# Up and down projections in three 256-column products per k-tile, and short matmuls ahead of chosen units

## The reference

```python
h = rmsnorm(x, norm_mix)
parts = split(h @ w_in)                      # 2048 x 14612: three mixers and gates
y_a, y_b, y_c = deltanet(..), mlstm(..), stick_breaking(..)
merged = gate_a * (y_a @ wb_a) + gate_b * (y_b @ wb_b) + gate_c * (y_c @ wb_c)
x = x + merged @ w_out
x = x + cross_attention(rmsnorm(x), rmsnorm(mem))   # wq, wkv, wo, four heads
up = causal_dwconv(rmsnorm(x) @ w_up, w_conv)       # 2048 x 11264, width 3
g, u = split(up)
out = x + (silu(g) * u) @ w_down                    # 5632 x 2048
```

## Time and profile before

| | |
|---|---|
| median of 3 runs | 2000.78 us (1995.47 to 2001.36) |
| profiled execution, its time | 2001.66 us |
| its span, first to last instruction | 1999.8 us |
| mean granted TensorE clock | 0.999 |
| TensorE busy | 1985.7 us, 99% |
| VectorE busy | 1216.7 us, 61% |
| ScalarE busy | 891.6 us, 45% |
| HBM traffic | 191 GB/s over the span |

### The profile page before, as it was taken

One profiled execution on the slowest core, in us unless ns is written; L12 is line 12 of the kernel. 1 busy time (PEld: TensorE's weight loads), 2 busy tenths in 40 slices (PEclk: granted clock), 3 DMA queues, 4 the chain that ended last, 5 costly groups with the idle time before them and its releaser, 6 DMA issues.

```text
span 1999.8 us, 34706 instructions
## 1 busy us (share of the span) xinstructions
PE 1985.7 (99%) x14790; PEld 1895.3 (95%) x14790; DVE 1216.7 (61%) x1352; ACT 891.6 (45%) x877; POOL 40.3 (2%) x62
## 2 busy tenths in 40 slices
PE   8999999999999999999999999999999999999999
PEld 8999999999999999999999999888888888888888
DVE  5677645445454476676655345777777777754444
ACT  5445434434374333455434444544444444433333
POOL 1000100000000000000000000000000000000000
PEclk9999999999999999999999999999999999999999
DMA  8665744665557756565554455665656565567564
GB/s 268 212 200 196 226 159 143 211 198 169 181 167 267 238 190 217 177 196 170 191 187 127 151 165 190 214 207 173 204 174 204 175 202 176 176 205 223 185 203 134
DMA packets 356636, 382.65 MB, mean 191 GB/s; under 512 B 8143, under 2 KB 351603, under 8 KB 355123
## 3 DMA queue, kind: packets, MB, share of 16 engines
q1 hardware_dynamic: 350947, 353.36, 55.3%
q0 software_dynamic: 5584, 27.70, 3.9%
HBM read 367.47 MB, written 13.58 MB: 191 GB/s over the span
## 4 chain that ended last, share of the span: by engine, by line
PE 98%; DVE 1%; ACT 0%; DMA 0%; issue 0%; SPq 0%; DVEq 0%; ACTq 0%
PE bank L1970 19%; PE bank L1971 18%; PE bank L1972 18%; PE bank L2009 16%; PE bank L2011 8%; PE bank L2485 8%; PE bank L2486 4%; PE bank L2392 1%; PE bank L2411 1%; PE bank L2169 1%; DVE w_lo_home L1139 0%; PE bank L2215 0%; PE bank L2072 0%; PE bank L2163 0%; DMA ident<-in_shape_masks 0%; PE bank L2281 0%
## 5 line engine op out<-in xcount | busy, mean ns | idle before, releaser
L1139 DVE TENSOR_TENSOR w_lo_home<-raw,w_hi_home 128x2048 fp32r<-128x2048 f32 (+1 forms) x349 | 757.0, 2169 | 604.5 <-ACT w_hi_home L547 604.2
L547 ACT ACTIVATE w_hi_home<-raw 128x2048 fp32r<-128x2048 f32 (+2 forms) x359 | 644.8, 1797 | 1047.0 <-PE bank L1972 627.6
L1970 PE MATMUL bank<-x_home,w_hi_home 128*128 128x256 f32 x2304 | 648.8, 282 | 2.0 <-DVE w_lo_home L1139 1.9
L1972 PE MATMUL bank<-x_home,w_lo_home 128*128 128x256 f32 x2304 | 644.4, 280 | 0.0
L1971 PE MATMUL bank<-x_home,w_hi_home 128*128 128x256 f32 x2304 | 644.4, 280 | 0.0
L2009 PE MATMUL bank<-x_home,w_hi_home 128*128 128x512 f32 x1408 | 488.5, 390 | 0.1
L1970 PEld LDWEIGHTS bank<-x_home,w_hi_home 128*128 128x128 f32 x2304 | 435.1, 189 | 2.9 <-issue 1.4
L1972 PEld LDWEIGHTS bank<-x_home,w_lo_home 128*128 128x128 f32 x2304 | 437.0, 190 | 0.0
L1971 PEld LDWEIGHTS bank<-x_home,w_hi_home 128*128 128x128 f32 x2304 | 433.1, 188 | 0.2
L2011 PE MATMUL bank<-x_home,w_lo_home 128*128 128x256 f32 x1408 | 397.1, 282 | 0.0
L2009 PEld LDWEIGHTS bank<-x_home,w_hi_home 128*128 128x128 f32 x1408 | 264.2, 188 | 55.5 <-issue 0.4
(11 more groups left out here) (315 smaller groups left out, 1946.4 us busy)
## 6 DMA issues: line engine op xcount, KB each, us to landing
raw<-in_w_in SPq DMA_DIRECT2D x52, 2048.0 KB, 8.5
raw<-in_ffn_up SPq DMA_DIRECT2D x44, 2048.0 KB, 7.9
raw<-in_ffn_down SPq DMA_DIRECT2D x32, 1408.0 KB, 6.9
raw<-in_xa_wkv SPq DMA_DIRECT2D x16, 2048.0 KB, 9.2
raw<-in_w_br SPq DMA_DIRECT2D x8, 2048.0 KB, 8.3
raw<-in_w_out SPq DMA_DIRECT2D x8, 2048.0 KB, 8.3
raw<-in_xa_wq SPq DMA_DIRECT2D x8, 2048.0 KB, 8.3
raw<-in_xa_wo SPq DMA_DIRECT2D x8, 2048.0 KB, 8.4
```

The costliest lines, as they stand in the source:

```text
L547: return nc.scalar.activation(out_, in_, func, **kw)
L1139: tt(split_out(w_lo, kind, half, at), halves(raw, kind, half, par), split_out(w_hi, kind, half, at).bitcast(f32), ALU.subtract).then_inc(l ...
L1970: mm(o, w[0], x[0], start=start, stop=False)
L1972: return mm(o, w[1], x[0], start=False, stop=stop)
```

## The change

UP and DN compute each k-tile as the other phases do, with `three` into the first 256 columns of the bank, and their weights are put at element 24. `minor`, its copy, the second addition in `finish` and `finish_last`, and three semaphores are gone; the scaling by `rstd` reads PSUM directly. Beside this, a short matmul (`lead_in`) is issued ahead of chosen half units. It multiplies the half unit's first weights and activations and is overwritten by the unit's first product. It has two sizes: `LEAD_WIDE`, 128 stationary and 2 moving columns, and `LEAD_SMALL`, 4 stationary and 16 moving. `SETTLE` is the wide one ahead of a unit's first half and the small one ahead of its second. A pair stands in A (half units 8 and 9), GA (its half units 6 and 7), GC unit 0, BR unit 0, one unit at each of the two calls of `norm_beside` (in WO and K), XO unit 1, UP units 3, 17 and 31, and each of the eight blocks of DN (block 0 ahead of its first unit, the others ahead of their third, after the transposes, with `bank[5]` as the place). BO unit 0 has the small one alone. These are 37 short matmuls.

```diff
-W_OF = {"UP": 0, "DN": 0, "V": 16}
+W_OF = {"V": 16}
+LEAD_WIDE, LEAD_SMALL = (P, 2), (4, 16)
+SETTLE = (LEAD_WIDE, LEAD_SMALL)
+UP_SETTLES = (3, 17, 31)
...
-        minor = sb("minor", [P, 2, SEQ], f32, d_scope)
...
-            def minor_part(j, up):
-                ...
-                for x in range(2):
-                    last = copy(minor[:, x, :], up_bank(par, x)[:, SEQ:2 * SEQ])
-                last.then_inc(f_minor, 1)
...
             def scale_tokens(j, up):
-                dve.wait_ge(f_minor, j * 2 + up + 1)
...
                 for x in range(2):
-                    last = tt(scaled[:, x * SEQ:(x + 1) * SEQ], up_bank(par, x)[:, 0:SEQ], minor[:, x, :], ALU.add)
+                    last = tt(scaled[:, x * SEQ:(x + 1) * SEQ], up_bank(par, x)[:, 0:SEQ], rstd[:, :], ALU.mult)
                 last.then_inc(dve_evac, 1)
-                dve.wait_ge(dve_evac, j * 2 + evacuated("UP", up)[1])
-                tt(scaled.rearrange("p (c s) -> p c s", c=2), scaled.rearrange("p (c s) -> p c s", c=2),
-                   bc(rstd[:, :].unsqueeze(1), [P, 2, SEQ]), ALU.mult).then_inc(f_scaled, 1)
...
             def finish_last(x):
-                tt(part, bank[1 + 2 * x][:, 0:SEQ], x_back[:, 2 * c + x, :], ALU.add).then_inc(dn_main, 1)
-                dve.wait_ge(dn_main, c + 1 + x)
-                tt(part, bank[1 + 2 * x][:, SEQ:2 * SEQ], part, ALU.add).then_inc(dve_evac, 1)
+                tt(part, bank[1 + 2 * x][:, 0:SEQ], x_back[:, 2 * c + x, :], ALU.add).then_inc(dve_evac, 1)
...
+            def lead_in(o, w, x, shape):
+                m, n = shape
+                return mm(o[0:m, 0:n], w[:, 0:m], x[:, 0:n], start=True, stop=True)
...
-                    for k in range(KC if name == "UP" else 0):
-                        ...
-                        mm(o[:, :].rearrange("p (j s) -> p j s", j=2), w_hi_home[:, half, at:at + P], acts[:, :, k, :],
-                           start=k == 0, stop=False)
-                        last = mm(o[:, SEQ:2 * SEQ], w_lo_home[:, half, at:at + P], acts[:, 0, k, :], start=False, stop=k == KC - 1)
+                    out_of = lambda g: up_bank(par, half)[:, 0:SEQ] if name == "UP" else bank[par + 2 * g][:, half * SEQ:(half + 1) * SEQ]
+                    if lead:
+                        lead_in(out_of(0), w_hi_home[:, half, place_of(name):], acts[:, 0, 0, :], lead)
...
             def norm_beside(k, m, acts):
-                product_half(m, acts)
-                product_half(m + 1, acts)
-                product_half(m + 2, acts)
+                leads = dict(zip((m + m % 2, m + m % 2 + 1), SETTLE))
+                for j in range(3):
+                    product_half(m + j, acts, lead=leads.get(m + j))
...
             for m in range(4, 14):
-                product_half(m)
+                product_half(m, lead={8: LEAD_WIDE, 9: LEAD_SMALL}.get(m))
...
+            project("BO", x_hl, 0, 1, leads=(LEAD_SMALL, None))
+            project("GC", x_hl, 0, 1, leads=SETTLE)
+            project("BR", y_hl, 0, 1, leads=SETTLE)
+            project("XO", x_hl, 1, 2, leads=SETTLE)
...
-            project("UP", x_hl, 1)
+            project("UP", x_hl, 1, UP_SETTLES[0])
+            for i, j in zip(UP_SETTLES, UP_SETTLES[1:] + (COUNT["UP"],)):
+                project("UP", x_hl, i, i + 1, leads=SETTLE)
+                project("UP", x_hl, i + 1, j)
...
             def down_pair(c, par):
+                settled = 0 if isinstance(c, int) and c == 0 else 2
...
-                            mm(o[:, :].rearrange("p (j s) -> p j s", j=2), w_hi_home[:, half, at:at + P], x, start=g + k == 0, stop=False)
-                            last = mm(o[:, SEQ:2 * SEQ], w_lo_home[:, half, at:at + P], x[:, 0, :], start=False,
-                                      stop=g * DG + k == FC - 1)
+                            if k == 0 and g == settled:
+                                lead_in((o if g == 0 else bank[5])[:, 0:SEQ], w_hi_home[:, half, at:], x[:, 0, :], SETTLE[half])
+                            w = [t[:, half, at:at + P] for t in (w_hi_home, w_lo_home)]
+                            last = three(o[:, 0:SEQ], w, [x[:, 0, :], x[:, 1, :]], g + k == 0, g * DG + k == FC - 1)
```

More of the change, by code:

```diff
@@ L1093, in _ @@
             hi_half(*half_of(first_half("DN") + 1))
-            minor_part(FC // 2 - 1, 1)
             silu_gate(FC // 2 - 1)
@@ L1940, in finish @@
                               x_back[:, bass.ds(c * 2 + x, 1), :].rearrange("p c s -> p (c s)"), ALU.add)
[L1941 to L1944, removed]
                 last.then_inc(dve_evac, 1)
@@ L1985, in wait_bank, with half_unit @@
                     pe.wait_ge(evac[e], i + (n - 2))
-            def half_unit(name, i, par, hp, half, acts, ready=None, passed=None, parts=None, ks=range(KC)):
+            def half_unit(name, i, par, hp, half, acts, ready=None, passed=None, parts=None, ks=range(KC), lead=None):
                 kind = kind_of[name]
@@ L2001, in half_unit @@
                     cuts = (0, GH, GH + MH, KC) if kind == BR else (0, KC)
-                    for k in range(KC if name == "UP" else 0):
[L2003 to L2008, removed]
-                        mm(o[:, :].rearrange("p (j s) -> p j s", j=2), w_hi_home[:, half, at:at + P], acts[:, :, k, :],
-                           start=k == 0, stop=False)
-                        last = mm(o[:, SEQ:2 * SEQ], w_lo_home[:, half, at:at + P], acts[:, 0, k, :], start=False, stop=k == KC - 1)
-                    for k in ks if name != "UP" else ():
+                    out_of = lambda g: up_bank(par, half)[:, 0:SEQ] if name == "UP" else bank[par + 2 * g][:, half * SEQ:(half + 1) * SEQ]
+                    if lead:
+                        lead_in(out_of(0), w_hi_home[:, half, place_of(name):], acts[:, 0, 0, :], lead)
+                    for k in ks:
                         if parts and k == KC // 2:
@@ L2018, in half_unit @@
                         w = [t[:, half, k * P:(k + 1) * P] for t in (w_hi, w_lo)]
-                        last = three(bank[par + 2 * g][:, half * SEQ:(half + 1) * SEQ], w, [acts[:, j, k, :] for j in range(2)],
+                        last = three(out_of(g), w, [acts[:, j, k, :] for j in range(2)],
                                      k == cuts[g], k + 1 == cuts[g + 1])
@@ L2026, in half_unit, with product_half @@
                     last.then_inc(half_used, 1)
-            def product_half(m, acts=x_hl, ready=None, passed=None, parts=None, ks=range(KC)):
+            def product_half(m, acts=x_hl, ready=None, passed=None, parts=None, ks=range(KC), lead=None):
                 name, i, par, hp, half = half_of(m)
@@ L2032, in product_half, with project @@
                     wait_bank(name, i)
-                half_unit(name, i, par, hp, half, acts, ready, passed, parts, ks)
-            def project(name, acts, start=0, stop=None):
+                half_unit(name, i, par, hp, half, acts, ready, passed, parts, ks, lead)
+            def project(name, acts, start=0, stop=None, leads=(None, None)):
                 def unit(i, par, hp):
@@ L2038, in unit @@
                     for half in range(2):
-                        half_unit(name, i, par, hp, half, acts)
+                        half_unit(name, i, par, hp, half, acts, lead=leads[half])
                 stop = COUNT[name] if stop is None else stop
@@ L2192, in _ @@
             product_half(m + 5)
-            product_half(m + 6)
+            product_half(m + 6, lead=LEAD_WIDE)
             m += 7
-            for _ in range(2 * FIRST_LEVEL - 1):
-                product_half(m)
+            for j in range(2 * FIRST_LEVEL - 1):
+                product_half(m, lead=None if j else LEAD_SMALL)
                 m += 1
@@ L2273, in _ @@
                 to_features(bank[3 + j], j, lambda h, a: S_T[:, a * GH + h, :], y_t)
-            for name in ("BQK", "BV", "BO"):
+            for name in ("BQK", "BV"):
                 project(name, x_hl)
+            project("BO", x_hl, 0, 1, leads=(LEAD_SMALL, None))
+            project("BO", x_hl, 1)
             def scores(b, k, q):
@@ L2347, in _ @@
             product_half(m + 7)
-            project("GC", x_hl)
+            project("GC", x_hl, 0, 1, leads=SETTLE)
+            project("GC", x_hl, 1)
             pe.wait_ge(y_lo, 4)
-            project("BR", y_hl)
+            project("BR", y_hl, 0, 1, leads=SETTLE)
+            project("BR", y_hl, 1)
             m = first_half("WO")
```

12 lines of the change are left out of this document (2 added, 10 removed).

## The result

The changed kernel took 1976.59 us in the median (1975.33 to 1978.79, four runs) against 2000.65 us (1995.47 to 2001.36): 24.1 us faster, a ratio (of the means) of 0.9886 with a 95% interval of 0.9868 to 0.9905. Forecast were 1972 us and a range of 1963 to 2010. The profiled execution took 1976.82 us, its span is 1974.9.

What follows compares the result with a forecast made beforehand. TensorE, 99% busy, was taken as the bound: matmul count times start-to-start distance. Terms -14.3 - 19.0 + 3.7 - 0.4 = -30.0 us from the profiled 2001.66 us gave 1972 us, range 1963 to 2010.

Steps and rivals of the forecast that it cites:

- Two paces that are set by what stands ahead, and then kept: TensorE's stream: 113.2 or 117.7 ns per 256-column matmul; a short block can set either pace, and what follows keeps it.
- The sign that I named, 0.34 us right behind each short matmul: In the changed kernel's stretches, k-tiles of 0.34 us, the fast pace, were to stand right behind each short matmul.
- rival 3: Each short matmul only turns the pace over, so about half the k-tiles are fast: -6.2 us, 1995 us; chance 0.10.
- UP and DN, forecast -14.3 us: Three products instead of two at the fast pace, 339.5 against 346.6 ns: 2016 k-tiles x -7.1 ns = -14.3 us.
- The other half units, forecast -19.0 us: Outside UP and DN, 88 slow halves of 48 matmuls turn fast, 4.5 ns per matmul: -19.0 us, bounds -15.3 and -22.7.
- the 71 halves counted as sure: Slow halves in A, GA, BO, CQK, GC, BR, WO, K and XO, following a pair with only products between: -15.3 us.
- the 34 behind single sums: Halves in WO, K and Q behind single 256-column sums; effect unknown, bounds all and none, so half, 17, were counted.
- The short matmuls, 0.10 us each: The 37 short matmuls lie on TensorE's path: 37 x 0.10 = +3.7 us, bounds 0 and +7.0 us.
- Rival 1: Fast pace only where already seen, with `x_home` as operand, not with `y_hl`, `mem_hl`, `act_hl`: -11.6 us, 1990 us; chance 0.13.
- Rival 2: Short matmuls don't set the pace; UP and DN run slow over 2112 k-tiles: +17.2 us, 2019 us; chance 0.20.
- Its even point, f = 0.60: Rival 2 with no gain elsewhere: 2112 x (6.6 - 13.7 f) + 3.3 = 0; said to decide once over half are slow.
- ScalarE and VectorE, forecast at nothing: Dropped copy and additions, 30 us of VectorE, worth nothing as TensorE never waited; one tail addition fewer, -0.4 us.

Runs made afterwards that it cites:

- experiment 5: The changed kernel with only the pair at XO unit 1, no other short matmuls: 2002.43 us, ratio 1.0012 to the kernel before.
- experiment 6: The changed kernel with one pair in UP, at unit 1, instead of three, and none in DN: 1996.74 us, ratio 0.9989 to the kernel before.
- experiment 9: The changed kernel with one pair in UP, at unit 2, and BO's and A's short matmuls moved: 1978.13 us, ratio 0.9896 to the kernel before.
- experiment 10: The changed kernel with one UP pair, at unit 2, BO's and A's short matmuls moved, no DN pairs: 1973.97 us, ratio 0.9875 to the kernel before.
- experiment 1: The changed kernel without any of its 37 short matmuls, three products kept: 1983.98 us, ratio 0.9925 to the kernel before.
- experiment 2: The kernel before with 15 short matmuls, none in UP and DN, which keep two products per k-tile: 1988.17 us, ratio 0.995 to the kernel before.
- experiment 3: The kernel before with all 37 short matmuls, two products per k-tile and weights at element 0 in UP and DN: 1990.63 us, ratio 0.9961.
- experiment 11: The changed kernel again, unaltered, beside two variants on the same chip: 1977.94 us, ratio 0.9897 to the kernel before.

## Why the prediction was right, and where it was off

**Two paces that are set by what stands ahead, and then kept.** Right for what short matmuls and the sums do, and confirmed at single steps and by experiments 5, 6, 9 and 10. "Kept" needs a limit: waits and single late starts ended the fast pace in some executions and not in others. The sign that I named, 0.34 us right behind each short matmul, holds for the small one alone. What I had not said is that the outcome depends on the pace before: the small one turns it over, so rival 3 describes the small one alone, and the wide one in front is what makes the pair come out the same from either side.

**UP and DN, forecast -14.3 us.** In the profiled executions, the way from the sums to the end of the span went from 729.9 to 721.1 us, -8.8; forecast were -14.3, +2.2 for 22 short ones and -0.4, -12.5 in all. The term that was mis-sized is this one. Slow k-tiles that I had not counted: 64 in UP units 1 and 2, taken as even though the sums leave them slow (64 x 6.6 ns = 0.4 us), and the half unit behind each wide one, 3 x 16 in UP and 8 x 11 in DN, 136 x 13.7 ns = 1.9 us. With a fall between 1755 and 1770 us and 22 x 0.01 us more for the short ones this makes some 3 of the 3.7 us. The rest is in the price: two matmuls taken off each count made the fast k-tile 339.5 ns, while its starts in the traces give 340.0, so that a k-tile is worth 6.6 ns and not 7.1, 1.0 us over 2016, which covers what is left. Experiment 1 shows the products without pairs: from the sums to the last matmul 712.2 us against 726.9, of which 0.4 us is the shorter tail; to the start of the last product 711.2 against 725.4, -14.2 us, where the 2080 k-tiles behind the sums give -14.8 at 7.1 ns and -13.7 at 6.6.

**The other half units, forecast -19.0 us.** With the 15 short ones there at 0.10 us that is -17.5; the profile shows the sums of UP at 1253.7 instead of 1269.9 us, -16.1. By medians it is less, -10.6 in experiment 2, since the profiled execution of before lay near the slow end of its runs. Of the 71 halves counted as sure, A's 6 and BO's 5 did not come; of the 34 behind single sums, where I took half, nearly all did. These two misses have opposite signs, and that the term came out so near is in part luck.

**The short matmuls, 0.10 us each from the earlier trace rows.** Measured 0.11 us, twice. What they cost beside it, a half unit at the slow pace behind each wide one, was in no term of the sum.

**The rivals.** Rival 1 fell: BR with `y_hl`, K with `mem_hl` and DN with `act_hl` all run at 113 ns. Rival 2 said that without an effect of the pairs UP and DN run slow, at 2019 us. That step was wrong as a statement about UP and DN: without any pairs they ran fast, 1984 us, because the long sums happened to turn the pace the right way. Its prices hold: in experiment 5 1508 of the 2112 k-tiles ran slow, and the way from the sums to the last matmul is 732.5 us, 20.3 above experiment 1, where 1508 x 13.7 ns gives 20.7. Its even point, f = 0.60, is the share of fast k-tiles, so it decides once more than 0.4 of them are slow, not half. The Trainium skill ("TensorE: Matmul & The Clock Gate", section "Back-to-back issue gap") gives a matmul's columns at 2.4 GHz and 2.5 ns as the gap of a matmul taken by itself, and says that in a stream the weight loads set the distance too. By that formula 256 columns would be 109.2 ns, an estimate, and three products 2.5 ns more than two. The traces agree that a stream is not bound by it: 113.3 or 117.8 ns, and 768 columns in three products took 340.0 ns, in two 346.6, which is the other direction.

**ScalarE and VectorE, forecast at nothing.** Consistent with TensorE's waits for weights, 3.0 us in three places instead of 1.9 in two. The tail's 0.4 us came: from the start of the last product to the end of the span it is 4.53 us before and 4.08 after, 4.49 and 4.50 in experiments 2 and 3, which keep the second addition, and 4.04 to 4.08 in 1, 5, 6, 9, 10 and 11, which don't.

## What to carry to other kernels

When one engine is busy all the time, divide stretches of its time by the count of its instructions before counting instructions: here one stream ran at 113.3 or 117.7 ns, and 16,000 matmuls times 4.5 ns is more than any single edit gave. A pace that is kept from its start makes distant edits interact, so judge an edit by the pace in each stretch and not by the total, and look at what stands directly behind each foreign block. Where a wait stands in the stream, one trace doesn't settle the pace behind it. And test "the added thing does it" by leaving it out: without the pairs in DN the kernel was faster.

## What the runs showed of the hardware

- A stream of 128 x 128 x 256 matmuls on hi and lo parts has two steady start-to-start distances, 113.3 and 117.8 ns, at the same granted clock of 1.00; with V's weights at element 16 there is a third, 116.7. The pair of a 512-column and a 256-column matmul has one, 346.3 to 347.0 ns by the counts, in the three traces that have it, all with the weights at element 0.
- The fast distance lasted for 6268 matmuls with seven blocks of transposes between (experiment 1), and in CQK through a wait of 1 us in nine traces of thirteen; in the other four it ended there. In K one start 0.03 to 0.04 us late ended it in three traces of eleven.
- A short matmul of 4 stationary and 16 moving columns turned the distance over each time that it met products of known pace, 140 times.
- One short matmul between products costs 0.11 us, and with 16 moving columns its stationary width went with the distance that follows a slow stretch: 4, 32 and 64 columns led to the fast one, 8, 16 and 96 to the slow one, mostly seen once or twice each. Why, no run here tells. What inside TensorE holds the two states stays open, and so does whether the third product or the place of the weights lets UP and DN have the fast one; neither was tried by itself.
